# Constants behind the projection slabs, channel transposes ahead of the fourth modulation product, and their scaling on two engines

## The chip, the cores and the metric

One core of a Trainium2 chip runs one program that holds both blocks of the model. The metric is the device time of one execution in microseconds. Three executions of the kernel before took 1608.85, 1611.86 and 1614.03 us; the median is 1611.86 us.

## The reference

The first block is a transformer layer with an adaptive modulation; the second block has two layers of its own and follows on its output. Only the opening of the first block bears on the change:

```python
mod(c) = silu(c) @ w_mod + b_mod      # 1024 -> 6 x 1024: sh1, sc1, g1, sh2, sc2, g2
h      = rms(x, norm1) * (1 + sc1) + sh1      # x: 256 tokens x 1024, by c
hc     = rms(ctx, norm1) * (1 + csc1) + csh1  # ctx: 256 tokens, by c_ctx
p      = h @ w_in                             # 1024 -> 2064, the same for hc
# p is split into a Fourier part, attention q, k, v, a gated delta rule's q, k, v (through a
# 3-tap convolution over time and silu), its output gate, and 16 gate columns
```

After the projections come the Fourier mixing, the attention, the bidirectional delta rule, the output projection and the MLP (1024 to 4096 and back), then the second block. All inputs and the output are float32.

## The kernel before, in words

The program is written by hand, one instruction stream per engine, with semaphores between them. Weights come through a ring of four slots (`ring`), each of 128 x 4096 floats (2 MB); SyncE's queue fills them (L1855 to L1864). The order of the slabs in `first_units` is mod0 to mod3, in2, in3, in0, in1, mod4 to mod11, out0, out1, and then the MLP's. A slot is filled again when the products that read it are done (`release`).

The small inputs are issued by ScalarE at its start, L2248 to L2254: the vectors, the rows, the shared constants `ca` (128 x 2306 floats; the identity, a rotation, cosines, masks and `pick`, in that order), x, ctx, the first block's constants `cb` (1472 KB: discrete Fourier matrices, cumulative sums, masks), and the 16 gate columns of w_in (`tail3`).

PSUM has eight banks. Every result that goes through a bank is a job. `first_jobs` lists the jobs in the order in which TensorE writes them; job n takes bank (4 + n) mod 8, and before it is written the reader of the bank's old job must be through (`Writer.open`). Each job has one engine that reads and empties it; an engine's `Reader` counts the jobs that it emptied on a semaphore of its own, `emptied[who]`. There are three such counters before: dve, act and gate.

The opening runs as follows, with the lines of the kernel before:

- TensorE multiplies silu(c) and silu(c_ctx) with a modulation slab (`mod(u)`, L1888). ScalarE copies the product to SBUF (L2268), TensorE turns it into channel columns with `pick` (`mod_T(u)`, L1896), and VectorE adds the bias (L2509). Slabs 0 and 1 give the shift sh1, slabs 2 and 3 the scale sc1.
- Meanwhile ScalarE squares and sums x and ctx (L2274), GpSimd makes the inverse roots (L2439, L2442), and ScalarE multiplies (L2282): x_hat and ctx_hat, signalled by `hat_ready`. The copies of mod1 to mod3 stand behind these on ScalarE.
- After all four slabs TensorE transposes x_hat and ctx_hat, 128 channels at a time, eight jobs hT0 to hT7 of four transposes (L1918).
- VectorE makes `ab` = norm1 * (1 + sc1) (L2516, L2517), waits for `cb`, and writes hT = hT * ab + sh1, two instructions for each job, one for x and one for ctx (L2522). It empties all eight.
- TensorE waits for the last of them and multiplies the projections: conv0 to conv5 (the delta rule's q, k, v; L1927), dz0 and dz1, `gates`, in0_0 and on. conv0 and conv1 are 256 tokens wide, conv2 to conv5 512. ScalarE copies each conv product out (L2300), and VectorE convolves it (L2543 to L2546).

## Time and profile before

| | |
|---|---|
| median of three runs | 1611.86 us |
| profiled execution | 1609.46 us |
| its span | 1607.7 us |
| TensorE busy (share of the span) | 1483.1 us (92%) |
| VectorE busy | 881.7 us (55%) |
| ScalarE busy | 687.8 us (43%) |
| GpSimd busy | 83.1 us (5%) |
| mean granted TensorE clock | 0.954 |

A busy share says how much of the span an engine works, not which engine others wait for; that is read from the waits, the timeline and the chain, stretch by stretch. PE is TensorE's matmul, PEld its weight load, DVE VectorE, ACT ScalarE, POOL GpSimd, SP SyncE; a q behind a name is the engine's own issuing. PEclk is the granted TensorE clock, 1.00 for 2.4 GHz and 0.50 for 1.2 GHz.

### The profile page before, as it was taken

The page shows a single profiled execution, that of the slowest core. Times are in us where ns is not written, and L with a number is a line of the kernel's source. Part 1 is how long each engine was busy: PE and PEld are TensorE (multiplying, and loading weights), DVE is VectorE, ACT ScalarE, POOL GpSimd, SP SyncE. Part 2 cuts the span into 40 slices and gives each one's busy share as a digit, 9 for nine tenths or more (in the row PEclk, how much of TensorE's full clock was granted, in tenths as well). Part 3 has the DMA queues.
Part 4 walks back from the last instruction along what each step waited for, and adds up shares of the span by engine and source line. Part 5 has one row for each costly group of instructions (what it writes and reads, how often), then busy time and mean ns, then how long its engine had stood idle before and what let it go on. Part 6 is the DMA issues. An engine that isn't in the chain of part 4 may idle for free. (4 is left out here: it accounts for less than half of the span.)

```text
span 1607.7 us, 27054 instructions
## 1 busy us (share of the span) xinstructions
PE 1483.1 (92%) x11287; PEld 1254.8 (78%) x11287; DVE 881.7 (55%) x1366; ACT 687.8 (43%) x1152; POOL 83.1 (5%) x87
## 2 busy tenths in 40 slices
PE   3898699999899999999988999998999989999996
PEld 1565677765799979988886999987989887799985
DVE  0543724252655555557677555565647768555555
ACT  3012222542444434457743444453437673344442
POOL 0000473000000000000000000000000000000000
PEclk8889789999999999999999999999999999999998
DMA  9522056001545425533324754533743332755420
GB/s 355 204 89 105 2 202 221 2 2 61 199 166 202 157 80 178 170 106 106 105 106 145 274 196 170 195 106 95 194 151 106 105 106 105 269 202 201 167 102 27
DMA packets 120895, 230.35 MB, mean 143 GB/s; under 512 B 20064, under 2 KB 34528, under 8 KB 120032
## 3 DMA queue, kind: packets, MB, share of 16 engines
q1 hardware_dynamic: 117776, 221.37, 39.6%
q10 hardware_dynamic: 3024, 7.64, 1.3%
q8 instruction: 69, 1.13, 0.3%
q14 instruction: 26, 0.21, 0.0%
HBM read 227.95 MB, written 1.05 MB: 142 GB/s over the span
## 5 line engine op out<-in xcount | busy, mean ns | idle before, releaser
L745 DVE TENSOR_TENSOR work_rounded<-ring,work_rounded 128x1024 fp32r<-128x1024 f32 x208 | 240.8, 1219 | 102.1 <-ACT work_rounded L737 101.9
L708 PE MATMUL psum<-channels_rounded,work_rounded 128*128 128x256 f32 x2048 | 285.8, 286 | 0.3 <-DVE work_rounded L775 0.3
L708 PEld LDWEIGHTS psum<-channels_rounded,work_rounded 128*128 128x128 f32 x2048 | 271.7, 195 | 3.9 <-issue 2.5
L719 PE MATMUL psum<-work_rounded 128*128 128x512 f32 x1152 | 265.7, 390 | 0.0
L961 PE MATMUL psum<-channels_rounded,ring_rounded 128*128 128x256 f32 x1728 | 254.7, 290 | 2.3 <-PEq L2799 1.2
L737 ACT ACTIVATE work_rounded<-ring 128x1024 fp32r<-128x1024 f32 x208 | 203.1, 1050 | 121.4 <-PE psum L719 118.5
L719 PEld LDWEIGHTS psum<-work_rounded 128*128 128x128 f32 x1152 | 214.8, 188 | 43.5
L961 PEld LDWEIGHTS psum<-channels_rounded,ring_rounded 128*128 128x128 f32 x1728 | 228.5, 196 | 9.2 <-issue 7.9
L1429 DVE TENSOR_TENSOR ring_rounded<-ring,ring_rounded 128x1024 fp32r<-128x1024 f32 x80 | 94.3, 1197 | 48.9 <-ACT ring_rounded L1233 48.2
L785 DVE TENSOR_TENSOR work<-work 128x512 f32<-128x512 f32 x48 | 33.2, 692 | 109.2 <-ACT work L757 109.2
L757 ACT ACTIVATE work<-psum 128x512 f32<-128x512 f32 x48 | 28.7, 598 | 139.8 <-PE psum L708 139.8
L1233 ACT ACTIVATE ring_rounded<-ring 128x1024 fp32r<-128x1024 f32 x80 | 80.7, 1026 | 11.1 <-DMA ring<-in_w_in 11.1
L2010 PEld LDWEIGHTS psum<-work 64*64 64x64 f32 x1840 | 58.1, 138 | 22.5 <-issue 20.9
L2010 PE MATMUL psum<-work 64*64 64x64 f32 x1840 | 61.6, 223 | 13.0 <-issue 7.6
L708 PE MATMUL psum<-work_rounded 128*128 128x256 f32 x256 | 73.1, 286 | 0.0
L961 PE MATMUL psum<-channels_rounded,work_rounded 128*128 128x256 f32 x384 | 69.0, 283 | 0.0
L2258 ACT ACTIVATE work<-psum 128x512 f32<-128x512 f32 (+1 forms) x75 | 43.5, 580 | 50.0 <-PE psum L2010 27.1
L1429 DVE TENSOR_TENSOR ring_rounded<-ring,work_rounded 128x1024 fp32r<-128x1024 f32 x46 | 53.9, 1219 | 18.8 <-ACT work_rounded L1233 18.7
L961 PEld LDWEIGHTS psum<-channels_rounded,work_rounded 128*128 128x128 f32 x384 | 58.8, 188 | 2.0 <-DVE ring_rounded L1429 0.7
L1233 ACT ACTIVATE work_rounded<-ring 128x1024 fp32r<-128x1024 f32 x46 | 45.2, 1050 | 29.7 <-DMA ring<-in_w_in 24.0
L1401 POOL TENSOR_SCALAR small<-small 128x1 f32<-128x1 f32 x8 | 5.8, 728 | 970.9 <-DVE small L1634 970.9
L1888 PE MATMUL psum<-ring,small 128*32 128x512 f32 x192 | 29.2, 736 | 24.7 <-DMA ring<-in_w_mod 24.7
(365 smaller groups left out, 2078.8 us busy)
## 6 DMA issues: line engine op xcount, KB each, us to landing
ring<-in_w_in SPq DMA_DIRECT2D x20, 2048.0 KB, 8.5
ring<-in_w_ff SPq DMA_DIRECT2D x16, 2048.0 KB, 8.4
ring<-in_w_ff_in SPq DMA_DIRECT2D x16, 2048.0 KB, 7.8
ring<-in_w_ff_out SPq DMA_DIRECT2D x16, 2048.0 KB, 8.1
ring<-in_w_mod SPq DMA_DIRECT2D x12, 2048.0 KB, 8.9
ring<-in_w_out SPq DMA_DIRECT2D x6, 2048.0 KB, 8.1
ring<-in_w_in SPq DMA_DIRECT2D x8, 1024.0 KB, 5.5
ring<-in_w_up SPq DMA_DIRECT2D x4, 2048.0 KB, 8.0
```

Of the source, the lines that this page charges most:

```text
L708: mm = pe.matmul(psum[:, 4 + 2 * half + q, i * SEQ:(i + 1) * SEQ], w1[pw][:, k, m * P:(m + 1) * P], y[py][:, k, :], start=((k, n) == (0, 0 ...
L719: mm = pe.matmul(psum[:, 2 * t + n, :], h[ph][:, kq, t * P:(t + 1) * P], w2[pw][:, kq, n * 512:(n + 1) * 512], start=False, stop=False, sk ...
L737: act.activation(parts.high[i % 2][:, at], ring[:, SLOT * s + 1024 * c:SLOT * s + 1024 * (c + 1)], ACT.Copy).then_inc(w_high, 1)
L745: dve.tensor_tensor(parts.low[i % 2][:, at], ring[:, SLOT * s + 1024 * c:SLOT * s + 1024 * (c + 1)], exact(parts.high[i % 2][:, at]), ALU. ...
L757: act.activation(parts.h[q], v3(psum[:, 4 + i, :], SEQ), ACT.Relu).then_inc(hid_raw, 1)
L785: dve.tensor_tensor(h, h, h, ALU.mult).then_inc(hid_sq, 1)
L961: mm = pe.matmul(ps[:, at:at + SEQ], u[pw][:, k, col:col + P], y_parts[py][:, k, :], start=((k, n) == (0, 0)), stop=((k, n) == (KC - 1, 2)))
L1233: act.activation(piece(high_of.get(name, high_slot), name, c), piece(raw(name), name, c), ACT.Copy).then_inc(piece_high, 1)
L1429: dve.tensor_tensor(piece(low_of(name), name, c), piece(raw(name), name, c), exact(piece(high_of.get(name, high_slot), name, c)), ALU.subt ...
L1888: mm = pe.matmul(ps[strip, :], cs3[:, k, :], wu[:, k, :], start=(k < 4), stop=(k >= 4))
L2010: mm = pe.matmul(ps[half(c), 256 * d + h * HD:256 * d + h * HD + HD], lhs[d][half(c), at], rhs[d][half(c), at], start=True, stop=True)
L2258: r.read(name, act.activation(dst, r.open(name, width), ACT.Copy))
```

## The change

Four things are done. ScalarE issues only the first 130 columns of the shared constants (the identity, and `pick`, which moves to second place in the table); the other columns and the first block's constants are issued on SyncE's queue behind slab in1, and their wait moves to the `gates` product and to VectorE's reading of it. The transposes of channel jobs hT0 to hT5 are written before mod3, hT6 and hT7 after its transpose. Each job has a reader by its number: VectorE scales the even ones, ScalarE the odd ones with an activation of function Identity with a scale and a bias per partition; two new counters, `even` and `odd`, and a semaphore `ab_ready` order this. conv0 waits for each channel job in front of the K step that reads it, instead of for the last one in front of all.

```diff
--- before.py
+++ after.py
@@ -76,9 +76,9 @@
     chunked = np.where(c[None, :] <= c[:, None], 0.0, NEG)
     dsa = np.concatenate([chunked, np.zeros((P, P)), chunked], axis=1)
     return {
-        "ident": eye, "rot": rot, "cosT": np.cos(ang), "sinT": np.sin(ang), "causal": wide, "sb_neg": sb,
+        "ident": eye, "pick": ((i[:, None] % 32) == np.arange(2)[None, :]) * 1.0, "rot": rot, "cosT": np.cos(ang), "sinT": np.sin(ang), "causal": wide, "sb_neg": sb,
         "chunked": dsa, "after": (i[:, None] > i[None, :]) * 1.0, "upto": (i[:, None] <= i[None, :]) * 1.0,
-        "ones": np.ones((P, P)), "pick": ((i[:, None] % 32) == np.arange(2)[None, :]) * 1.0,
+        "ones": np.ones((P, P)),
     }
 
 
@@ -142,7 +142,7 @@
 
 
     def __init__(self):
-        self.all, self.by_name, self.counts = [], {}, {"dve": 0, "act": 0, "gate": 0}
+        self.all, self.by_name, self.counts = [], {}, {"dve": 0, "act": 0, "gate": 0, "even": 0, "odd": 0}
         self.in_bank = {}
 
     def add(self, name, by, wide=False, bank=None):
@@ -211,10 +211,16 @@
         for name in names:
             j.add(name, by, wide=True)
 
+    def channels_in(chunks):
+        for c in chunks:
+            add("odd" if c % 2 else "even", f"hT{c}")
+
     for u in range(4):
+        if u == 3:
+            channels_in(range(6))
         add("act", f"mod{u}")
         add("dve", f"modT{u}")
-    add("dve", *(f"hT{c}" for c in range(KC)))
+    channels_in((6, 7))
     add("act", *(f"conv{c}" for c in range(6)), "dz0", "dz1")
     add("dve", "gates")
     add("act", "in0_0", "in0_1")
@@ -445,7 +451,8 @@
         unit_in = [sem(f"unit_in{s}") for s in range(RING)]
         consts_in = sem("consts_in")
         products_done = sem("products_done")
-        emptied = {"dve": sem("dve_emptied"), "act": sem("act_emptied"), "gate": sem("gate_emptied")}
+        emptied = {"dve": sem("dve_emptied"), "act": sem("act_emptied"), "gate": sem("gate_emptied"),
+                   "even": sem("even_emptied"), "odd": sem("odd_emptied")}
         dve_step, act_step, pool_step = sem("dve_step"), sem("act_step"), sem("pool_step")
         w_high, w_low = sem("w_high"), sem("w_low")
         split_used = sem("split_used")
@@ -475,10 +482,10 @@
         first_sems = [sem(n) for n in ("qk_ready", "g_ready", "conv_ready", "l2_ready", "L_ready", "A_ready", "X_ready",
                                        "vk_ready", "S_zero", "dn_ready", "x1_ready", "gate_in", "conv_out",
                                        "conv_silu", "conv_exp", "e2_done", "decay_in", "decay_done", "pads_zero",
-                                       "rows_through", "ident_in", "MT_ready", "XT_ready", "eg_steps", "rden_ready")]
+                                       "rows_through", "ident_in", "ab_ready", "MT_ready", "XT_ready", "eg_steps", "rden_ready")]
         (qk_ready, g_ready, conv_ready, l2_ready, L_ready, A_ready, X_ready, vk_ready, S_zero, dn_ready, x1_ready,
          gate_in, conv_out, conv_silu, conv_exp, e2_done, decay_in, decay_done, pads_zero, rows_through,
-         ident_in, MT_ready, XT_ready, eg_steps, rden_ready) = first_sems
+         ident_in, ab_ready, MT_ready, XT_ready, eg_steps, rden_ready) = first_sems
         loop_sems = [products_done, *emptied.values(), dve_step, act_step, pool_step, w_high, w_low, split_used, y_split, hid_sq,
                      hid_high, y_in,
                      inputs_in, tail_in, params_in, sums_ready, scales_ready, silu_in, silu_c, hat_ready,
@@ -1862,6 +1869,9 @@
                         u = int(name[3:] if name[:3] in ("mod", "out") else name[2:])
                         w = wm({"mod": "w_mod", "out": "w_out"}.get(name[:3], "w_in"))
                         load(name, w[:, :, 512 * u:512 * (u + 1)])
+                        if name == "in1":
+                            sp.dma_start(cb, a["first_consts"]).then_inc(consts_in, 16)
+                            sp.dma_start(ca[:, 130:], a["shared_consts"][:, 130:]).then_inc(consts_in, 16)
                     mlp_loads(sp, q, wm("w_ff1"), wm("w_ff2"), release)
                     ahead = q_layer[0]
                     sp.wait_ge(w_low, CHUNKS * 13)
@@ -1904,31 +1914,38 @@
                         return mm
 
                     pe.wait_ge(silu_c, 1)
+
+                    def channels_in(chunks):
+                        for c in chunks:
+                            ps = w.open(f"hT{c}")
+                            for t in range(4):
+                                src = (hat3 if t < 2 else ctx3)[:, t % 2, c * P:(c + 1) * P]
+                                mm = pe.transpose(ps[:, t * P:(t + 1) * P], src, ident)
+                            w.done(mm)
+
                     for u in range(4):
+                        if u == 3:
+                            pe.wait_ge(hat_ready, 1)
+                            channels_in(range(6))
                         mod(u)
                         if u == 0:
                             pe.wait_ge(ident_in, 16)
                         mod_T(u)
-                    pe.wait_ge(consts_in, 16)
-                    pe.wait_ge(hat_ready, 1)
-                    for c in range(KC):
-                        ps = w.open(f"hT{c}")
-                        for t in range(4):
-                            src = (hat3 if t < 2 else ctx3)[:, t % 2, c * P:(c + 1) * P]
-                            mm = pe.transpose(ps[:, t * P:(t + 1) * P], src, ident)
-                        w.done(mm)
-                    w.after(f"hT{KC - 1}")
+                    channels_in((6, 7))
 
                     for c in range(6):
                         u = landed(f"in{2 + c // 4}")
                         n = SEQ if c < 2 else 512
                         ps = w.open(f"conv{c}")
                         for k in range(KC):
+                            if c == 0:
+                                w.after(f"hT{k}")
                             mm = pe.matmul(ps[:, 0:n], u[:, k, (c % 4) * P:(c % 4 + 1) * P], hT[:, k, 0:n],
                                            start=(k == 0), stop=(k == KC - 1))
                         w.done(mm)
                     for t in range(TT):
                         w.done(tokens(w.open(f"dz{t}"), u, 256, 256, t))
+                    pe.wait_ge(consts_in, 32)
                     pe.wait_ge(tail_in, 16)
                     ps = w.open("gates")
                     for t in range(4):
@@ -2247,10 +2264,9 @@
                     r = Reader(act, j1, "act", step)
                     act.dma_start(vecs, a["vecs"]).then_inc(params_in, 16)
                     act.dma_start(rows, a["rows"].to_broadcast([P, ROW_N])).then_inc(params_in, 16)
-                    act.dma_start(ca[:, :], a["shared_consts"]).then_inc(ident_in, 16)
+                    act.dma_start(ca[:, 0:130], a["shared_consts"][:, 0:130]).then_inc(ident_in, 16)
                     act.dma_start(x3, a["x"][0].rearrange("(t p) d -> p t d", p=P)).then_inc(inputs_in, 16)
                     act.dma_start(ctx3, a["ctx"][0].rearrange("(t p) d -> p t d", p=P)).then_inc(inputs_in, 16)
-                    act.dma_start(cb, a["first_consts"]).then_inc(consts_in, 16)
                     act.dma_start(tail3, wm("w_in")[:, :, 2048:2064]).then_inc(tail_in, 16)
                     act.preload_act_table_set("natural_log_exp_and_others")
 
@@ -2284,6 +2300,15 @@
                             last.then_inc(hat_ready, 1)
                     for u in range(1, 4):
                         mod_copy(u)
+                    act.wait_ge(ab_ready, 1)
+                    odd = Reader(act, j1, "odd", step)
+                    for c in range(1, KC, 2):
+                        ps = odd.open(f"hT{c}")
+                        for s in range(2):
+                            last = act.activation(hT[:, c, SEQ * s:SEQ * (s + 1)], ps[:, SEQ * s:SEQ * (s + 1)],
+                                                  ACT.Identity, bias=modT[:, 2 * c + s:2 * c + s + 1],
+                                                  scale=ab[:, 2 * c + s:2 * c + s + 1])
+                        odd.read(f"hT{c}", last)
 
                     def conv_exp_minus(c):
 
@@ -2515,14 +2540,15 @@
                     r.settle()
                     do(dve.tensor_scalar(ab, modT[:, 16:32], 1.0, None, ALU.add))
                     do(dve.tensor_tensor(v3(ab, 2), v3(ab, 2), spread(vec("norm1"), 2), ALU.mult))
-                    dve.wait_ge(consts_in, 16)
-                    for c in range(KC):
-                        ps = r.open(f"hT{c}")
+                    dve.sem_inc(ab_ready, 1)
+                    even = Reader(dve, j1, "even", step)
+                    for c in range(0, KC, 2):
+                        ps = even.open(f"hT{c}")
                         for s in range(2):
                             last = dve.tensor_scalar(hT[:, c, SEQ * s:SEQ * (s + 1)], ps[:, SEQ * s:SEQ * (s + 1)],
                                                      ab[:, 2 * c + s:2 * c + s + 1],
                                                      modT[:, 2 * c + s:2 * c + s + 1], ALU.mult, ALU.add)
-                        r.read(f"hT{c}", last)
+                        even.read(f"hT{c}", last)
 
 
                     dve.wait_ge(pads_zero, 1)
@@ -2552,6 +2578,7 @@
                     dve.sem_inc(conv_ready, 1)
 
 
+                    dve.wait_ge(consts_in, 32)
                     ps = r.open("gates", 64)
                     g4 = lambda ap, at: v3(ap, 16)[:, :, at:at + 8].rearrange("p t (d h) -> p d t h", d=2)
                     out4 = lambda ap: ap.rearrange("p (d t h) -> p d t h", d=2, t=4)
```

## Rows read from the trace of the kernel before

**Rows 1.** Waits of TensorE, whole span: for whom, us in total, times, longest.

```profile
PE psum L1888 <- DMA ring<-in_w_mod: 24.7, 4, 15.3
...
PE psum L1945 <- DVE small L2573: 3.4, 1, 3.4
```

**Rows 2.** Timeline, 0 to 75 us: start, duration, engine, line, operation [idle before].

```profile
1.85 0.60 ACTq L2250 DMA_DIRECT2D shared_consts<-in_shared_consts  x1
...
8.71 0.22 ACT L2261 ACTIVATE small<-small 128x16 f32<-128x16 f32 x1 [2.64 <-DMA work<-in_rows]
...
15.33 3.20 PE L1888 MATMUL psum<-ring,small 128*32 128x512 f32 x16 [15.33 <-DMA ring<-in_w_mod]
...
18.59 0.60 ACT L2268 ACTIVATE work<-psum 128x512 f32<-128x512 f32 x1 [9.57 <-PE psum L1888]
...
20.17 1.06 ACT L2274 ACTIVATE work<-x_tok 128x1024 f32<-128x1024 f32 x1 [0.98 <-DMA work<-in_ctx]
...
28.38 2.17 ACT L2282 ACTIVATE work<-work,small 128x1024 f32<-128x1024 f32 x2
...
31.63 0.60 ACT L2268 ACTIVATE work<-psum 128x512 f32<-128x512 f32 x1 [1.09 <-PE psum L1888]
...
32.28 1.05 PE L1896 MATMUL psum<-shared_consts,work 128*128 128x2 f32 x8 [0.80 <-ACT work L2268]
...
33.59 1.92 PE L1888 MATMUL psum<-ring,small 128*32 128x512 f32 x16 [0.25 <-DMA ring<-in_w_mod]
...
35.66 0.60 ACT L2268 ACTIVATE work<-psum 128x512 f32<-128x512 f32 x1 [3.43 <-PE psum L1888]
...
39.01 3.30 PE L1888 MATMUL psum<-ring,small 128*32 128x512 f32 x16 [1.65 <-DMA ring<-in_w_mod]
...
42.47 0.60 ACT L2268 ACTIVATE work<-psum 128x512 f32<-128x512 f32 x1 [6.21 <-PE psum L1888]
...
43.12 1.05 PE L1896 MATMUL psum<-shared_consts,work 128*128 128x2 f32 x8 [0.81 <-ACT work L2268]
...
44.03 3.69 PE L1918 MATMUL psum<-shared_consts,work 128*128 128x128 f32 x32
...
44.90 8.23 DVE L2522 TENSOR_SCALAR xT<-psum,small 128x256 f32<-128x256 f32 x16
...
53.19 22.00 PE L1927 MATMUL psum<-xT,ring 128*128 128x256 f32 x60 [5.46 <-DVE xT L2522]
59.82 0.39 ACT L2300 ACTIVATE work<-psum 128x256 f32<-128x256 f32 x1 [16.75 <-PE psum L1927]
...
63.27 0.39 ACT L2300 ACTIVATE work<-psum 128x256 f32<-128x256 f32 x1 [3.07 <-PE psum L1927]
```

**Rows 3.** DMA queues, 8 to 12 us, then 14 to 16: packets, MB, share.

```profile
q10 hardware_dynamic: 187, 1.30, 77.4%
q1 hardware_dynamic: 182, 0.37, 23.9%
...
q1 hardware_dynamic: 147, 0.28, 36.6%
```

**Rows 4.** DMA issues, 0 to 75 us: times, size of each, us to landing.

```profile
work<-in_first_consts ACTq DMA_DIRECT2D x1, 1472.0 KB, 20.8
shared_consts<-in_shared_consts ACTq DMA_DIRECT2D x1, 1153.0 KB, 10.4
```

**Rows 5.** Stretches: engines' busy time (instructions), PEclk, DMA share, GB/s.

```profile
38.00:39.00 1.00, 0.00 (x0) 0.00 (x0) 0.00 (x0) 0.00 (x0) 0.00 (x0) 0.72 1.06 391
41.00:42.00 1.00, 1.00 (x8) 0.00 (x0) 0.00 (x0) 0.00 (x0) 0.00 (x0) 0.58 1.04 383
...
47.70:52.00 4.30, 0.02 (x1) 0.00 (x0) 4.15 (x9) 0.00 (x0) 0.00 (x0) 1.00 1.05 387
52.00:53.00 1.00, 0.00 (x0) 0.00 (x0) 0.96 (x3) 0.00 (x0) 0.00 (x0) 0.54 1.05 385
58.00:59.00 1.00, 1.00 (x4) 0.77 (x3) 0.00 (x0) 0.00 (x0) 0.00 (x0) 0.54 1.06 389
```

## The prediction

> **What bounds the kernel now.** I read the page first, then the waits of TensorE over the whole span, the timeline of the first 75 us, the DMA issues and queues of that stretch, and the granted clock by the microsecond. TensorE is the busiest engine, and of all its waits only four are for a transfer, 24.7 us in sum; all four are for modulation slabs (w_mod) [rows 1] and lie in the first 40 us [rows 2]. So nothing after 40 us is paced by HBM, and after the projections begin TensorE runs on to its wait of 3.4 us for the gates [rows 1], whose VectorE chain hangs on TensorE's own products. A shift of the first projection product should therefore pass through to the end nearly whole.
>
> The stretch in front of it is not TensorE-bound. The product of slab 0 starts at 15.33 and its copy at 18.59. ScalarE's squares start at 20.17, released by the landing of ctx, and the last normalizing multiply ends at 28.38 + 2.17 = 30.55. Slabs 1 to 3 are multiplied as they land, slab 3 last, at 39.01. Its copy starts at 42.47, its transpose at 43.12, the eight channel transposes at 44.03. VectorE scales them from 44.90 for 8.23 us, TensorE idles 5.46 us, and conv0 starts at 53.19 at half clock and is copied out at 59.82 [rows 2]. That copy is my measuring point.
>
> **The transfers.** ScalarE's queue and SP's queue share the DMA engines packet by packet: in four microseconds the one passed 187 packets and 1.30 MB, the other 182 packets and 0.37 MB [rows 3]. A wide-rowed constant on the first queue so takes most of the bytes from the modulation slabs. The change takes 1087 of the 1153 KB of shared constants and all 1472 KB of the first block's constants out of this stretch (130 of the table's 2306-odd columns stay, 66 KB) [rows 4]. At the 383 to 391 GB/s of [rows 5] these 2.62 MB are 6.8 us.
> - ctx: the rows of parameters were in at 8.7 (8.71 ScalarE, released by them, [rows 2]) and the shared constants at 1.85 + 10.4 = 12.25 [rows 2, 4]: 3.55 us for the table. The piece left still passes 128 packets, each with a slab packet of 2 KB beside it (0.33 MB together, some 0.8 us by that rate); I take 1.0 us. ctx lands 2.6 us sooner, at 17.55. Bounds: 0 (the queue stays packet-bound) and 3.5.
> - slab 0 had to come 1.1 us sooner for its copy not to hold the squares: the copy ended at 19.2 [rows 2]. By the shares of [rows 3] the slab's queue moves 0.09 MB/us beside the wide rows and 0.14 beside x (0.28 MB in two microseconds); with the table gone slab 0 lands some 2 us sooner, so its copy ends by 17.1. It is just not in the way.
> - slab 3: 38.9 less about 6.3 is 32.6. TensorE gets there later than that, see below.
> - The moved constants go on SP's queue behind slab in1, whose issue waits for the fourth modulation product (four slabs fit the ring). Total bytes are unchanged and the DMA share stays full, so they land where the last slab did: four slabs of 2.1 MB at 388 GB/s behind slab 3, 39.0 + 4 x 5.4 = 60.6. Their first readers are the gates, behind conv0 (47.5 below), conv1 (3.45), four of double width (27.6) and dz0 and dz1 (6.9 by the same step): about 85.5. That wait, on TensorE and on VectorE, is passed some 25 us after the landing: nothing. With the cover gone, the gates' product, in0 and all behind them would stand. Behind the two transfers on SP's queue stands only the load of mod4, which waits for conv3, three products behind conv0: nothing.
>
> **The new chain.** The squares to the last multiply take 10.38 us: 17.55 + 10.38 = 27.95. Behind it on ScalarE stands the copy of mod1 (its product, slab landed near 22, is long done). Copy to transpose is 0.65 (31.63 to 32.28), transpose to the next product 1.05: mod2 starts at 29.7. A product to its copy is 2.07 at full clock (33.59 to 35.66) and 3.46 at half (39.01 to 42.47) [rows 2]. TensorE idles before it, so I take half: copy at 33.1, transpose at 33.8, channel transposes at 34.7 (0.91 later, 43.12 to 44.03). Six channel jobs of 3.69/8 = 0.46 are 2.8 us; they now stand in front of mod3 and wait for no scaling, since their banks were freed by earlier jobs. mod3 starts at 37.5, after its landing; at full clock its copy starts at 39.55, its transpose at 40.2, and scaling starts 1.78 later (43.12 to 44.90), at 42.0.
>
> Jobs hT6 and hT7 reuse the banks of hT0 and hT1, so they wait for the first scaling of each engine. VectorE's job takes 8.23/8 = 1.03: hT0 is through at 43.0, and TensorE's two transposed jobs at 44.0. VectorE has four jobs, to 46.1. ScalarE's four are eight activations of 128x256 from PSUM; the trace does not show this very operation, the nearest rows are 0.39 for a copy of that size [rows 2]. Bounds: 0.39 each and VectorE's own 0.51 (8.23/16); I take the 0.39 of the same engine, so 3.1 us, with the waits between some 3.6, hidden behind VectorE's 4.1; at 0.51 the two end level, and the waits would cost 0.2 us or so. No row shows Identity on ScalarE, so a table load cannot be excluded by rows alone: it would cost 1.28 for one load on this chain. In the Trainium skill, page "ScalarE: Activation LUTs", section "Table sets: the hidden batching unit", identity is one of the cheap functions in every set, by which that is 0; no run here shows it yet.
>
> conv0 now takes each job as it comes. A K step at full clock is 3.45/8 = 0.43 (59.82 to 63.27 for conv1): 44.0 + 3.45 = 47.5, later than 46.1 + 0.86 = 47.0. Against 59.82 that is 12.3 us. By parts: 3.0 from the sooner modulation chain (42.5 to 39.5), 4.1 from sharing, and the rest from conv0 overlapping the scaling and not running at half clock.
>
> **The clock.** It fell at 38.4, a microsecond after TensorE ran dry, rose at 41.8 after 2.8 us of slab 3's product; it fell at 52.1 in the idle before conv0 and rose at 58.9 [rows 5]. In the new order TensorE has 0.65 us dry before modT3, 1.8 us before hT6, and only short work between. That may drop the clock once near conv0. The short dip of before, 38.4 to 41.8, is 3.4 us and costs half of that, 1.7 us. I take one such dip: gain 12.3 - 1.7 = 10.6 us. Bounds: none, 12.3 (and 13.7 if mod2 too is at full clock), and conv0 wholly at half.
>
> A rule speaks against this order. The clock stayed full through the eight channel transposes and for 4.3 us behind them [rows 5]; so they at least did not lose it. The Trainium skill, "TensorE: Matmul & The Clock Gate", section "Part 4: PE-mode transpose", says transposes don't count as activity that brings the full clock. By it, transposes in front of mod3 would leave that product at half, which is the first half of the rival below; the trace neither confirms it nor refutes it.
>
> The sum stands against the profiled execution: 1609.5 us (span 1607.7), 2.4 below the median shown of 1611.9. 1609.5 - 10.6 = 1598.9 for such an execution, 1611.9 - 10.6 = 1601.3 for the median, which I forecast.
>
> **Rivals.**
> - No dip: gain 12.3 to 13.7, 1598.2 to 1599.6. For it: TensorE is busy from 33.8 on but for two short gaps. Against: two falls of the clock in this stretch followed gaps of that size.
> - Low clock through: six short transposes leave the clock low, mod3 runs at half (3.46 for 2.07: 1.4 more), conv0 too (8 x 0.86 for 8 x 0.43: 3.4 more). Gain 12.3 - 4.8 = 7.5: 1604.4. For it: conv0 at half clock before, for 5.7 us of steady work.
> - Transfers not sooner: the first landings are bound by packets, not bytes, and ctx still lands at 20.15. Everything is 2.6 later: gain 8.0, 1603.9. Against: the 3.55 us of the table. If both this and the low clock hold, gain 4.9, 1607.0.
> - The other side: conv products that start piecemeal don't bring the clock back. The six are 34.5 us of work at full clock (two of 3.45, four of double width), and what runs at half takes twice its time. The 12.3 us are spent once 12.3 us of this work, conv0, conv1 and most of conv2, have run at half; through conv3 (20.7 us) it would be 8.4 us slower, 1620. For it: only that conv0 starts at half. Against: before, the clock came back in 5.7 us of the same work.
> - That the change does less than it says: the even/odd sharing buys nothing if ScalarE's Identity is slow; only over 1.0 us per job of two would it pass VectorE, against 0.39 per copy.
>
> **From this to the numbers.** One dip 0.45, no dip 0.22, low clock through 0.14, transfers not sooner 0.08, both of these 0.07, slower 0.04. 0.3% is 4.8 us, about what a measurement of this kernel can tell from no change; so below 1607.0 is faster. Most of the case at 1607.0 and a little scatter of the others (the three runs before lie 5 us apart) fall within 0.3%: faster 0.88, same 0.08, slower 0.04. The range takes in no dip less 2 us of scatter and the low cases with it: 1596.5 to 1607.
>
> **What would show it.** Squares start near 17.6; the copy of mod1 near 28; mod3's product starts behind 24 transposes near 37.5 with no wait for its slab; scaling starts near 42 and both engines end near 46; conv0's copy near 47.5 to 50. The DMA share drops near 60 as before, and neither TensorE nor VectorE waits for constants at the gates. From conv1's copy to the end everything stands as far apart as before. The prediction is wrong if mod3 waits for its slab, if the squares still start at 19 or later, if ScalarE is the last to scale, or if a stage after the projections gets longer by more than 2 us.

## The result and the profile after

The changed kernel takes 1600.43 us, median of eleven runs, against 1611.86 us for eleven of the kernel before; the ratio is 0.9946 with a 95% interval of 0.9928 to 0.9964, 5.8 to 11.6 us less. The profiled execution took 1598.39 us with a span of 1596.6 us, 11.1 us less in the span than before. The forecast was 1601.3 us, faster. It is met, but the 11.1 us of this pair of traces are not where the forecast had put them: 7.6 us lie in front of conv0's copy (10.6 were forecast) and 3.5 us behind it (none were). The traced execution is the fastest of the eleven; e5 below traces one that is the slowest of six.

The timeline of the changed kernel, opening, answering to [rows 2] (start, duration, engine, line, operation, idle before):

```profile
12.74 3.64 PE L1898 MATMUL psum<-ring,small 128*32 128x512 f32 x16 [12.74 <-DMA ring<-in_w_mod]
...
17.53 1.06 ACT L2290 ACTIVATE work<-x_tok 128x1024 f32<-128x1024 f32 x1 [0.50 <-DMA work<-in_ctx]
...
27.82 0.57 ACT L2284 ACTIVATE work<-psum 128x512 f32<-128x512 f32 x1
28.45 1.62 PE L1906 MATMUL psum<-shared_consts,work 128*128 128x2 f32 x8 [3.16 <-ACT work L2284]
30.00 3.64 PE L1898 MATMUL psum<-ring,small 128*32 128x512 f32 x16
...
33.78 0.60 ACT L2284 ACTIVATE work<-psum 128x512 f32<-128x512 f32 x1 [5.39 <-PE psum L1898]
34.43 1.86 PE L1906 MATMUL psum<-shared_consts,work 128*128 128x2 f32 x8 [0.80 <-ACT work L2284]
36.16 4.19 PE L1923 MATMUL psum<-shared_consts,work 128*128 128x128 f32 x24
...
40.28 1.93 PE L1898 MATMUL psum<-ring,small 128*32 128x512 f32 x16
42.35 0.60 ACT L2284 ACTIVATE work<-psum 128x512 f32<-128x512 f32 x1 [7.97 <-PE psum L1898]
...
44.91 4.20 ACT L2308 ACTIVATE xT<-psum,small 128x256 f32<-128x256 f32 x8 [1.96 <-DVEq L2543]
44.97 4.10 DVE L2548 TENSOR_SCALAR xT<-psum,small 128x256 f32<-128x256 f32 x8 [0.15 <-DVE small L2542]
46.02 1.97 PE L1923 MATMUL psum<-shared_consts,work 128*128 128x128 f32 x8 [1.90 <-DVE xT L2548]
47.78 27.53 PE L1943 MATMUL psum<-xT,ring 128*128 128x256 f32 x78
52.22 0.39 ACT L2325 ACTIVATE work<-psum 128x256 f32<-128x256 f32 x1 [3.11 <-PE psum L1943]
```

The squares start at 17.53, 2.6 us sooner, and mod1's copy at 27.82. From there the chain is slower than forecast: the transpose of mod1, mod2 and modT2 and most of the 24 channel transposes run at half clock, and the transposes (36.16 to 40.28) stand squarely in front of mod3. Its slab is no longer waited for (issued at 9.2, it landed 23.4 us later, at 32.7): of the four waits for slabs of [rows 1] two are left, and they are those of slabs 0 and 1. The wait of TensorE for slabs, whole span (for whom, us in total, times, longest):

```profile
PE psum L1898 <- DMA ring<-in_w_mod: 15.4, 2, 12.7
```

Stretches of the changed kernel, answering to [rows 5] (busy time of each engine, then PEclk, DMA share, GB/s):

```profile
28.00:29.00 1.00, 0.55 (x4) 0.55 (x4) 0.00 (x0) 0.40 (x1) 0.00 (x0) 0.87 1.05 387
38.00:39.00 1.00, 1.00 (x7) 1.00 (x6) 0.00 (x0) 0.00 (x0) 0.00 (x0) 0.51 1.05 387
45.00:46.00 1.00, 0.00 (x0) 0.00 (x0) 0.97 (x2) 0.97 (x3) 0.00 (x0) 0.91 1.05 387
49.00:50.00 1.00, 1.00 (x5) 0.84 (x4) 0.07 (x1) 0.11 (x1) 0.00 (x0) 0.89 1.05 385
59.00:60.00 1.00, 1.00 (x4) 0.41 (x3) 0.89 (x2) 0.00 (x0) 0.00 (x0) 1.00 0.53 218
```

The clock (2.4 GHz at 1.00, 1.2 at 0.50) fell at 28.7, rose at 39.0, fell at 45.8 and rose at 49.2. Of the first stretch only mod2's share was forecast, the second was forecast whole. The moved constants, issued at 42.67 and 44.84 (DMA issues: size, us to landing), were in at 59.3 and 61.9, and nobody waited for them:

```profile
work<-in_first_consts SPq DMA_DIRECT2D x1, 1472.0 KB, 16.6
shared_consts<-in_shared_consts SPq DMA_DIRECT2D x1, 1088.0 KB, 17.1
```

From conv0's copy to the first product of `gates` both kernels take 37.56 us, to the hundredth. The 3.5 us begin with it. TensorE's timeline from there, before and then after:

```profile
97.38 11.40 PE L1936 MATMUL psum<-work,xT 128*128 128x16 f32 x64
108.62 16.41 PE L1902 MATMUL psum<-ring,xT 128*128 128x512 f32 x32
128.38 0.58 PE L1945 MATMUL psum<-small,work 128*128 128x16 f32 x2 [3.35 <-DVE small L2573]
```

```profile
89.78 10.18 PE L1953 MATMUL psum<-work,xT 128*128 128x16 f32 x64
99.80 15.98 PE L1912 MATMUL psum<-ring,xT 128*128 128x512 f32 x32
119.14 0.37 PE L1962 MATMUL psum<-small,work 128*128 128x16 f32 x2 [3.35 <-DVE small L2600]
```

From the first product of `gates` to what follows them are 11.24 us, then 10.02, for the same instructions. In both kernels the clock falls during them, at 99.9 and at 93.6, although TensorE is never idle; how much of the work then falls in the low stretch differs.

### The profile page after: what moved, and what is told of

Same layout as the page of the kernel before. It is cut to its first block and busy times, and to the rows that moved or that the text cites. A ratio compares the mean times of both kernels' runs of the same rounds, so it can differ in the third digit from the quotient of the medians.

```text
span 1596.6 us, 27056 instructions
## 1 busy us (share of the span) xinstructions
PE 1481.6 (93%) x11287; PEld 1253.0 (78%) x11287; DVE 877.3 (55%) x1358; ACT 691.6 (43%) x1160; POOL 83.0 (5%) x87
## 3 DMA queue, kind: packets, MB, share of 16 engines
HBM read 227.95 MB, written 1.05 MB: 143 GB/s over the span
## 5 line engine op out<-in xcount | busy, mean ns | idle before, releaser
L764 ACT ACTIVATE work<-psum 128x512 f32<-128x512 f32 x48 | 28.7, 598 | 139.7 <-PE psum L715 139.7
L794 DVE TENSOR_TENSOR work_rounded<-work,work_rounded 128x512 fp32r<-128x512 f32 x48 | 33.2, 693 | 33.5 <-ACT work_rounded L766 33.5
```

Of the source, the lines that this page charges most:

```text
L764: act.activation(parts.h[q], v3(psum[:, 4 + i, :], SEQ), ACT.Relu).then_inc(hid_raw, 1)
L794: dve.tensor_tensor(parts.h_low[:, 2 * q:2 * q + 2, :], h, exact(parts.h_high[:, 2 * q:2 * q + 2, :]), ALU.subtract).then_inc(hid_done, 1)
```

## The experiments

Three marks are read from each trace: when scaling starts, when conv0's copy starts, and what lies behind. "To couplings" is from the first product of `gates` to the first of the delta rule's couplings, "rest" from there to the end of the span. Times are us; the median is of timed runs (6 to 12 of each), the ratio is to runs of the kernel before beside them, and the interval is 95%. e1 to e4 ran on one chip, e5 to e8 on a second, e9 to e12 on a third; the kernel before had medians of 1610.0, 1610.1 and 1609.9 us there. Each trace is one execution, and of the kernel before there is one trace only.

```
run                       scaling  conv0   to       rest    span    median   ratio to before
                          starts   copy    coupl.
before                    44.90    59.82   74.84   1435.5  1607.7  1611.9
changed                   44.97    52.22   72.12   1434.7  1596.6  1600.4   0.9946 (0.9928-0.9964)
e1  transfers only        43.82    57.60   73.52   1435.5  1604.2  1606.7   0.9987 (0.9969-1.0005)
e2  all but transfers     49.28    56.87   73.45   1439.0  1606.9  1603.8   0.9962 (0.9943-0.9982)
e3  VectorE scales all    42.96    51.14   72.12   1435.0  1595.8  1603.9   0.9967 (0.9952-0.9982)
e4  transposes behind     39.51    45.77   70.44   1443.4  1597.2  1599.8   0.9932 (0.9910-0.9953)
e5  changed again         46.45    54.05   73.51   1438.3  1603.4  1600.1   0.9939 (0.9923-0.9955)
e6  TensorE kept busy     40.50    46.42   75.10   1435.3  1594.4  1598.7   0.9929 (0.9911-0.9946)
e7  conv0 waits for all   42.91    52.63   73.47   1432.3  1596.0  1604.7   0.9966 (0.9947-0.9984)
e8  e4 + copies on DVE    37.83    44.09   72.11   1439.2  1593.0  1596.7   0.9920 (0.9896-0.9944)
e9  e8 + kept busy        38.44    44.69   75.12   1435.5  1592.9  1595.9   0.9906 (0.9872-0.9941)
e10 e8, VectorE alone     41.66    50.70   74.93   1435.5  1598.7  1597.3   0.9922 (0.9898-0.9947)
e11 e8, old transfers     46.41    54.01   73.37   1438.8  1603.7  1604.9   0.9962 (0.9938-0.9985)
e12 e8 again              40.44    46.70   73.19   1440.8  1598.3  1597.0   0.9908 (0.9873-0.9943)
```

**The transfers alone (e1).** The kernel before with the constants behind in1 (`pick` and the waits moved as in the change):

```diff
+                        if name == "in1":
+                            sp.dma_start(cb, a["first_consts"]).then_inc(consts_in, 16)
+                            sp.dma_start(ca[:, 130:], a["shared_consts"][:, 130:]).then_inc(consts_in, 16)
...
-                    act.dma_start(ca[:, :], a["shared_consts"]).then_inc(ident_in, 16)
+                    act.dma_start(ca[:, 0:130], a["shared_consts"][:, 0:130]).then_inc(ident_in, 16)
```

> Only the transfers are moved (constants behind slab in1); order and scaling as before. Theory, terms that add: ctx lands near 17.6 and the modulation slabs 6 us sooner, so scaling starts near 42.2 instead of 44.9, still takes 8.2 us, and conv0's copy comes at 54 to 57 instead of 59.8: 3 to 6 us gained, 1605 to 1608 against 1611. Rival, the slabs are bound by packets or the order alone brings the gain: scaling stays at 44.9, 0 to 1 us gained.

Squares at 17.51, scaling at 43.82, conv0's copy at 57.60: 2.2 us gained there, below the 3 to 6 expected. The slabs came sooner, but the clock was low from 28.4 to 45.4, so mod2 and mod3 took 3.64 us each. In the timed runs the interval touches 1.0: alone this edit can't be told from no change.

**All but the transfers (e2).** The changed kernel with the constants back on ScalarE's queue.

> Everything of the change but the transfers: the constants stay on ScalarE's queue in their old places. Theory: the chain from ctx is the one of the changed kernel, 2.6 us later, so scaling starts at 47.6 and conv0's copy comes at 54.8: 5 us gained of the 7.6. Rival, slab 3 becomes the bound again (it lands at 38.9, and 24 transposes stand in front of its product anyway): then the same 47 to 48, so only a start of scaling past 49 would speak for a cost of the order itself.

Scaling at 49.28, conv0's copy at 56.87, 4.65 later than in the changed kernel's first trace and 2.8 later than in its second (e5); the medians differ by 3.4 to 3.7, with intervals that overlap. The squares started 2.85 later (20.38). By the mark set beforehand, scaling past 49 speaks for a cost of the order itself. Here 24 transposes took from 39.31 to 44.60, at half clock, while slab 3 lay ready. The sum of 47.6 had them at the changed kernel's 4.1 us, so part of what passed the mark is the clock's.

**VectorE scales all (e3).** ScalarE's reader of the odd jobs is taken out, and:

```diff
-                    even = Reader(dve, j1, "even", step)
-                    for c in range(0, KC, 2):
+                    readers = [Reader(dve, j1, "even", step), Reader(dve, j1, "odd", step)]
+                    for c in range(KC):
+                        even = readers[c % 2]
                         ps = even.open(f"hT{c}")
```

> The changed kernel, but VectorE alone scales all eight channel jobs (in order 0 to 7, the two counters kept). Theory, sharing is worth the 4.1 us that VectorE's row loses, less what conv0's overlap takes back: scaling 45.0 to 53.2, conv0's copy at 54 to 57 against 52.2: 2 to 5 us slower than the changed kernel. Rival, conv0 at half clock hides the scaling whichever engine does it: within 1 us of the changed kernel.

```profile
42.96 7.33 DVE L2540 TENSOR_SCALAR xT<-psum,small 128x256 f32<-128x256 f32 x16 [0.15 <-DVE small L2533]
...
51.14 0.39 ACT L2316 ACTIVATE work<-psum 128x256 f32<-128x256 f32 x1 [10.19 <-PE psum L1943]
```

From the start of scaling to conv0's copy 8.18 us, against 7.25 with both engines and a similar dip of the clock: sharing was worth 0.9 us in the changed kernel, not 4.1. VectorE alone took 7.33 us (8.23 in the kernel before), and the copy came 0.85 behind its end, so here the scaling is the limit. With both engines it is TensorE, which in the changed kernel has no wait from 46.02 on. The rival has it: with part of their work at half clock, conv0 and the two late transposes take nearly as long as VectorE alone. The timed runs lie 3.5 us above the changed kernel's, on another chip and with intervals that overlap; the traced execution is the fastest of twelve.

**The transposes behind modT3 (e4).** The list of jobs is changed in the same way.

```diff
-                        if u == 3:
-                            pe.wait_ge(hat_ready, 1)
-                            channels_in(range(6))
                         mod(u)
...
-                    channels_in((6, 7))
+                    pe.wait_ge(hat_ready, 1)
+                    channels_in(range(KC))
```

> The changed kernel, but all eight channel jobs are transposed behind mod3 and its transpose, as before the change. Theory: putting 24 transposes in front of mod3 costs their 4.2 us on the chain (mod3 36.2 instead of 40.3, since its slab lands near 32.6) and hides nothing, because behind modT3 they run faster (0.46 a job) than two engines scale (0.53 a job); scaling starts near 42.3 and conv0's copy comes at 48 to 50: 2 to 4 us faster than the changed kernel. Rival, the prediction's own reading that the front place takes them off the path: scaling starts near 42 but conv0 waits for the transposes, copy at 52 to 55, no faster or 3 us slower.

Its timeline:

```profile
34.88 1.92 PE L1896 MATMUL psum<-ring,small 128*32 128x512 f32 x16
...
38.52 3.69 PE L1921 MATMUL psum<-shared_consts,work 128*128 128x128 f32 x32
39.51 4.09 DVE L2544 TENSOR_SCALAR xT<-psum,small 128x256 f32<-128x256 f32 x8 [0.15 <-DVE small L2538]
...
45.77 0.39 ACT L2321 ACTIVATE work<-psum 128x256 f32<-128x256 f32 x1 [1.90 <-PE psum L1939]
```

mod3 starts at 34.88 instead of 40.28, scaling 0.99 us behind the first transpose, and conv0's copy comes 6.4 us sooner than in the changed kernel, 8.3 sooner than in its second trace. Behind modT3 the scaling of the first job can start while the others are transposed: TensorE makes a job in 0.46 us, and two engines need 4.1 us for eight. Some of the 6.4 is the clock, which was full from 33. e6 below, with the transposes in front and the clock full too, gives the place without the clock: there they take 2.74 us in front of mod3, and from mod3's start to conv0's copy it takes 10.55 us, here 10.89. The front place costs 2.7 us and gives back 0.3. The whole time hardly moved, though (1599.8, intervals overlap): behind the couplings this execution lost 8.7 us against the changed kernel's.

**The changed kernel again (e5).**

> The changed kernel once more, unaltered. Theory, the opening's gain is fixed and what lies behind conv0 varies with where the clock falls: squares at 17.5, mod1's copy at 27.8, conv0's copy between 50 and 55, and gates to the couplings (72.1 in the changed kernel, 74.8 before) anywhere in 70 to 75, the difference being half of the low-clock time in that stretch. Rival, the change itself saves the 3.5 us behind conv0: 72.1 again within 0.3, and the same low stretches at the same distances.

The same program has scaling 1.5 us later, the copy 1.8 later, 1.4 more to the couplings, 3.6 more in the rest, 6.8 in the span. Its 24 transposes took 5.36 us instead of 4.19, at half clock throughout:

```profile
36.42 5.36 PE L1923 MATMUL psum<-shared_consts,work 128*128 128x128 f32 x24
```

From `gates` on this execution is 4.9 us longer than the first of the same program, and 1.5 us longer than the kernel before. So the 3.5 us behind conv0 cannot be credited to the change. From conv0's copy to `gates` all fourteen traces of the table take 37.6 us, at full clock. From `gates` to the couplings the time goes with the low-clock time in it (15 to 27 us of it, 70.4 to 75.1 us, correlation 0.99), and the rest likewise (95 to 122 us of it, 1432.3 to 1443.4, correlation 0.94, 0.42 us for each).

**TensorE kept busy in its waits (e6).**

```diff
+                    def fill(ps, n):
+                        for _ in range(n):
+                            pe.matmul(ps[:, 0:P], ident, ident, start=True, stop=True)
...
                         ps = w.open(f"modT{u}")
+                        fill(ps, {0: 0, 1: 14, 2: 3, 3: 3}.get(u, 0))
                         w.after(f"mod{u}")
...
+                    fill(psum[:, j1.bank("mod3"), :], 8)
                     channels_in((6, 7))
```

> The changed kernel with products of the identity with itself in TensorE's waits of the opening: 14 before modT1, 3 before modT2 and modT3, 8 before hT6; nothing reads them. Theory, the 10.2 us and the 3.4 us of low clock in the opening cost 4.7 (modT1, mod2, modT2, transposes at half) and 1.7 us: with them gone scaling starts near 40.5 and conv0's copy comes near 46, 6 us sooner. Rival, the copies and scalings set the pace and not the clock: scaling at 43 or later and less than 2 us gained.

```profile
33.13 2.82 PE L1929 MATMUL psum<-shared_consts,work 128*128 128x128 f32 x24
35.87 1.92 PE L1898 MATMUL psum<-ring,small 128*32 128x512 f32 x16
...
40.50 4.09 DVE L2555 TENSOR_SCALAR xT<-psum,small 128x256 f32<-128x256 f32 x8 [0.15 <-DVE small L2549]
...
46.42 0.39 ACT L2332 ACTIVATE work<-psum 128x256 f32<-128x256 f32 x1 [1.80 <-PE psum L1950]
```

Scaling at 40.50 and the copy at 46.42, as expected from the terms (40.5, 46). The clock was at 1.00 from here to the gates. The transposes in front of mod3 cost 2.74 us at full clock, where they cost 4.12 at mostly half. But the low stretches behind were long (75.1 us to the couplings), and the median, 1598.7, is only 1.4 below e5's, with intervals that overlap.

**conv0 waits for all scalings (e7).**

```diff
+                    w.after("hT6")
+                    w.after("hT7")
...
-                            if c == 0:
-                                w.after(f"hT{k}")
```

> The changed kernel, but conv0 waits for hT6 and hT7 and with them for all channel jobs before its first K step. Theory, the overlap is worth most of conv0: it starts at the end of the scaling (4.1 us behind its start) instead of 2.8 behind it, 1.3 us later at one clock, and with 3 us of TensorE idle again conv0 runs wholly at half as before: copy 11 us behind the start of scaling against 7.25, 3.7 us slower. Rival, without the clock's part: 8 to 9 us, 1 to 1.5 us slower.

9.72 us from the start of scaling to the copy, against 7.25: 2.5 us, between the two. TensorE idled 1.22 us, not 3 (the late transposes fill the rest), and conv0 took the 5.5 us of a mostly half clock: the clock was low from 43.8 to 50.6, twice as long as in the changed kernel. So 1.2 us are the lost overlap, and the rest goes with the longer dip. The median is 4.6 above e5's on the same chip, with intervals that overlap.

**The copies of mod1 to mod3 on VectorE, transposes behind (e8).** On top of e4:

```diff
-        add("act", f"mod{u}")
+        add("dve" if u else "act", f"mod{u}")
...
-                    for u in range(1, 4):
-                        mod_copy(u)
...
                     for u in range(4):
+                        if u:
+                            ps = r.open(f"mod{u}")
+                            r.read(f"mod{u}", dve.tensor_copy(mod_rows, ps))
                         mod(u)
```

> Transposes all behind modT3 (as in the fourth run) and the copies of mod1 to mod3 on VectorE, so that they don't stand behind the normalizing multiplies. Theory, ScalarE's chain from ctx (squares, roots, multiplies, then mod1's copy at 27.8) sets the opening: with the copies off it mod1's copy comes at 25.3, mod2 starts near 27.9 (when its slab has just landed), scaling starts at 37 to 40 and conv0's copy comes at 43.5 to 47: 1 to 2.5 us ahead of the fourth run's 45.8, about 7 ahead of the changed kernel. Rival, the slabs bound it: mod2 and mod3 wait for their landings and nothing is gained over the fourth run.

```profile
25.48 0.69 DVE L2535 COPY work<-psum 128x512 f32<-128x512 f32 x1 [7.03 <-PE psum L1896]
...
37.83 4.10 DVE L2545 TENSOR_SCALAR xT<-psum,small 128x256 f32<-128x256 f32 x8 [0.15 <-DVE small L2539]
...
44.09 0.39 ACT L2319 ACTIVATE work<-psum 128x256 f32<-128x256 f32 x1 [1.89 <-PE psum L1939]
```

mod1's copy comes 2.3 us sooner than behind the multiplies, scaling 1.7 and conv0's copy 1.7 us sooner than in e4. With 1596.7 it is 3.4 us below the changed kernel on the same chip, with intervals that overlap.

**The same kept busy (e9)**, with `fill` before mod1 (15), mod2 (8), mod3 (6), and before each modT (3).

> The eighth run's kernel (transposes behind modT3, copies of mod1 to mod3 on VectorE) with products of the identity with itself in TensorE's waits: 15 before mod1, 8 before mod2, 6 before mod3, 3 before each of modT1 to modT3; nothing reads them. Theory, at full clock throughout the slabs become the bound: mod2 starts at its landing near 27.3, mod3 at its own near 32.7, scaling at 37.0 and conv0's copy at 43.3, only 0.8 ahead of the eighth run's single look (44.1), 3 ahead of it in executions where the clock is low for longer. Rival, the slabs land sooner than I think and the chain goes on shrinking: scaling at 35 or earlier.

```profile
33.73 1.92 PE L1902 MATMUL psum<-ring,small 128*32 128x512 f32 x16 [1.16 <-DMA ring<-in_w_mod]
```

mod3 waits for its slab again, which lands at 33.7, 1 us later than I had it (and than in e8, 32.7); scaling starts at 38.44, 1.4 behind the expected 37.0. This is the next bound: with full clock and the short chain the slabs set the opening. In its median (1595.9 against e12's 1597.0) it is not apart from the same kernel unfilled.

**VectorE alone in the shorter order (e10)**, e8 with the edit of e3.

> The eighth run's kernel, but VectorE scales all eight jobs. Theory, with TensorE at full clock and the transposes not waiting for banks the scaling is the bound between its start and conv0's copy: 8.2 + 0.9 = 9.1 us from one to the other, against 6.26 with both engines: 2.9 us slower. Rival, as in the third run (8.2 us there against 7.25): about 1 us, because low clock takes the pace over.

```profile
38.80 1.87 PE L1904 MATMUL psum<-shared_consts,work 128*128 128x2 f32 x8 [0.88 <-DVE work L2526]
40.53 6.61 PE L1921 MATMUL psum<-shared_consts,work 128*128 128x128 f32 x32
41.66 7.33 DVE L2537 TENSOR_SCALAR xT<-psum,small 128x256 f32<-128x256 f32 x16 [0.30 <-PE psum L1921]
...
46.98 13.51 PE L1939 MATMUL psum<-xT,ring 128*128 128x256 f32 x47
50.70 0.39 ACT L2310 ACTIVATE work<-psum 128x256 f32<-128x256 f32 x1 [22.77 <-PE psum L1939]
```

9.04 us from scaling to the copy against 6.26 in e4, e8 and e12: 2.8 us, the expected size, but not by the expected path. The clock was low from 19.2 to 46.5, so the transposes took 6.61 us where e4, e8 and e12 had 3.69 at full clock: 2.9 us. TensorE never waited between them and conv0's copy. VectorE was through at 48.99, 1.7 us before the copy, so a second engine would have gained nothing in this execution, and the match with 2.9 is luck. What sharing is worth in this order at full clock is not measured; an estimate from e3, where VectorE alone set the pace (7.33 + 0.85 = 8.18), less the 6.26, is 1.9 us. The timed runs don't show it (1597.3 against 1597.0).

**The old transfers in the shorter order (e11)**, e8 with the edit of e2.

> The eighth run's kernel, but the constants go on ScalarE's queue in their old places. Theory, with the shorter chain the landing of slab 3 (38.9 there) is the bound: mod3 starts at 39, scaling at 43.4 to 44.8, conv0's copy at 49.7 to 51: 6 to 7 us later than the eighth run, where in the second run the same edit cost the old order 3 to 5. Rival, ctx's landing alone passes through: 2.7 us later.

```profile
39.02 3.64 PE L1893 MATMUL psum<-ring,small 128*32 128x512 f32 x16
...
54.01 0.39 ACT L2317 ACTIVATE work<-psum 128x256 f32<-128x256 f32 x1 [2.07 <-PE psum L1936]
```

mod3 starts at 39.02, when its slab lands, and the copy comes at 54.01, 7.3 us behind e12's and 9.9 behind e8's; the medians differ by 7.9. The expected 6 to 7 left out that mod3, modT3 and most of the transposes then ran at half (clock low from 34.7 to 48.4). modT2, also at half, was itself only through at 38.9, so this trace alone does not separate the slab from the clock. By the medians the transfers are worth 7.9 us in this order and 3.4 to 3.7 in the changed one (e2), where the transposes stand between the slab and mod3; the intervals overlap in either pair, here by a hair.

**e8 once more (e12).**

> The eighth run's kernel once more, beside the other three of this call. Theory: slab 1's product at 21.7, its copy near 25.5, scaling between 37.8 and 40, conv0's copy between 44 and 47, whole time within 2 us of the eighth run's 1596.7 median. Rival, the eighth run was a lucky set of executions: median above 1599.

Scaling at 40.44, the copy at 46.70, median 1597.0. mod1's copy stands at 25.35 as in e8 (25.48), but the clock was low from 20.2 to 37.3, and conv0's copy comes 0.9 us behind e4's: the 1.7 by which e8 beat e4 did not come again. The two sets of e8 give 0.9920 and 0.9908 with intervals to 0.9944 and 0.9943, the two of the changed kernel 0.9946 and 0.9939. Some 3 to 4 us better by the medians, with intervals that overlap; it beats the kernel before in every set.

## Why the prediction was right, point by point

- *The transfers.* Right. ctx 17.5 (17.55 forecast), mod1's copy 27.8 (27.95), mod2 at 30.0 (29.7), constants in at 59.3 and 61.9 (60.6), no wait at the gates. That slab 3 would not be waited for held, and it landed at 32.7 (32.6, though the step from 6.8 to 6.3 us has no working). For slab 0 the prediction asks for 1.1 us; by its own numbers it is 1.6 (19.2 less 17.55), and slab 0's product started 2.6 us sooner.
- *The chain to scaling.* The failed step is "mod3 starts at 37.5": 40.28. mod1's transpose to mod2 took 1.55 for 1.05, mod2 to its copy 3.78 for 3.46, modT2 to the transposes 1.73 for 0.91, six transposed jobs 4.12 for 2.77, together 3.0 us: the clock stayed low to 39.0, where I had it back after mod2. Scaling began at 44.97 for 42.0. e6, with the clock held up, began at 40.50 (my 42.0 less the 1.4 of mod2 at full clock is 40.6), so the terms were right and their clock was wrong. The trace of before held the warning: [rows 5] begin at 38, but ahead of them the clock had been low for 10.2 us there too, from 21.4 to 31.6:

```profile
21.00:22.00 1.00, 0.00 (x0) 0.00 (x0) 0.00 (x0) 0.97 (x3) 0.00 (x0) 0.68 1.03 426
22.00:23.00 1.00, 0.00 (x0) 0.00 (x0) 0.00 (x0) 0.97 (x3) 0.00 (x0) 0.50 0.98 407
...
30.00:31.00 1.00, 1.00 (x8) 0.00 (x0) 0.00 (x0) 0.55 (x1) 0.00 (x0) 0.50 1.05 385
31.00:32.00 1.00, 0.48 (x4) 0.00 (x0) 0.00 (x0) 0.37 (x1) 0.00 (x0) 0.70 1.04 383
```

In the changed kernel the sooner chain put mod2, modT2 and 24 transposes into such a stretch.
- *The place of the transposes.* I costed them at 2.8 us in front of mod3 and did not ask what they had cost behind it. There they had cost next to nothing: moving them ahead gave back 0.3 us behind mod3 (e6 against e4, both at full clock). They cost 2.7 us in front at full clock and 5.3 at half (e5, 36.42 to 41.71). At the mark of conv0's copy the reordering is a loss, and the rest of the change pays for it; in the whole time the loss is not shown, e4's interval overlaps the changed kernel's.
- *Sharing.* The 4.1 us by which VectorE's row shrinks were counted whole; 0.9 was their worth in the changed kernel (e3), and e10's 2.8 in the shorter order is the clock's. ScalarE's pace was under-rated too: 4.20 us for its four jobs, 0.56 for one instruction where I took 0.39. By that it was the last to scale, at 49.11 against VectorE's 49.07, which the prediction had named as a sign of being wrong; the 0.04 us cost nothing, since TensorE waited for neither after 46.02.
- *From scaling to conv0's copy.* 5.5 plus one dip of 1.7 was forecast, 7.2; it took 7.25, with the dip at 45.8 to 49.2. e4, e8 and e12 without one took 6.26, and e6, in the changed kernel's order, 5.92. So the 5.5 was 0.4 short and the dip cost 1.3, not 1.7: two misses that cancel.
- *The gain there.* 12.3 less 3.0 less 1.7 is 7.6, as measured. In size that is the rival of a clock low throughout (7.5), but not by its path: mod3 ran at full clock (1.93 us).
- *Behind conv0* I forecast no change. This pair of traces has 3.5 us there; with e5 in place of the first trace, the gain is 5.8 us at conv0's copy and 1.5 us are lost behind it. e5 shows that one program differs by as much from execution to execution, so the forecast stood as an expectation, and the nearness of 11.1 to 10.6 in one pair is partly luck. The timed ratio, 5.8 to 11.6 us, holds the 7.6. Whether the opening alone makes the 11.4 us between the medians stays open.
- *The Trainium skill's rule on transposes* ("TensorE: Matmul & The Clock Gate", "Part 4: PE-mode transpose": they don't count as activity for the full clock) is not borne out here. In the changed kernel the clock rose at 39.0 inside the 24 transposes, and mod3, which by that rule would have run at half, took 1.93 us, the full clock. In e10 it had been low from 19.2 through three modulation products and rose at 46.5, inside the 32 transposes that began at 40.53:

```profile
46.00:47.00 1.00, 1.00 (x9) 1.00 (x8) 1.00 (x3) 0.00 (x0) 0.00 (x0) 0.73 1.02 377
```

- *No table load for Identity*, as the Trainium skill, "ScalarE: Activation LUTs", "Table sets: the hidden batching unit", has it: the trace agrees, the changed kernel has two loads as before, at 4.4 and 598.0 us, neither at the scaling. ScalarE's group of loads in the opening (busy, mean ns, idle before):

```profile
L2271 ACT ACT_TABLE_LOAD x1 | 1.3, 1283 | 4.4 <-issue 4.4
```

## What to carry to other kernels

Before a step is moved ahead of another, ask what covers it where it stands: the 24 transposes cost 0.3 us behind the modulation and 2.7 to 5.3 in front of its last product. A row that shrinks (8.2 to 4.1 us of scaling) is worth only what the next limit leaves, and an earlier transfer is worth only what its reader still waits for when it lands. When a difference comes out as forecast, check that the engine it is laid to was the one waited for: e10's 2.8 us were the clock's. Where one trace differs from another by a few us, read a mark close behind the edit, and run the same program twice before crediting what lies far behind it.

## What the runs showed of the hardware

- The same program differed by 6.8 us in its span between two traces (e5); the low-clock stretches differ in place and length, and the time behind `gates` goes with them.
- TensorE's being busy was not enough to keep its clock: in `gates`, 64 products of 16 columns back to back, it fell at 93.6 in the changed kernel (PEclk over that microsecond 0.80, TensorE busy throughout), and 2.5 to 4.9 us behind the first of them in every one of the fourteen traces:

```profile
93.00:94.00 1.00, 1.00 (x9) 1.00 (x9) 0.00 (x0) 0.00 (x0) 0.00 (x0) 0.80 1.05 410
```

- The modulation products (weight loads of 128x32) don't bring it back reliably either: in e1 and e10 two and three of them ran at 3.64 us with the clock low in and between them.
- Before the first recorded change the granted clock reads 1.00, but the first product took 3.64 us, what it takes at 0.50, against 1.92 at full clock. At the very start the durations decide, not that column.
